# Hybrid attention and recurrence block on one core: token sums of the Strassen-Winograd up product formed after the turning instead of before it, with three small moves

## The reference

```
u = rmsnorm(h) * attn_norm_w
proj = u @ w_in                 # q,k,v of 8 attention heads; q, two gates, v, g of 4 recurrent heads
mix = concat(neighbourhood_attention(...), hgrn2_bidirectional(...))
h = h + mix @ w_out
u = rmsnorm(h) * mlp_norm_w
a = square(relu(u @ w_up))      # 1024 -> 4096
h = h + a @ w_down              # 4096 -> 1024
```

## Time and profile before

| what | value |
|---|---|
| median of 3 runs | 1293.55 us (1292.2 to 1294.88) |
| profiled execution | 1293.81 us, span 1292.0 us |
| TensorE busy | 1274.4 us, 99% |
| VectorE busy | 845.6 us, 65% |
| ScalarE busy | 587.4 us, 45% |
| GpSimd busy | 473.9 us, 37% |
| granted TensorE clock | 1.000 |

### The profile page before, as it was taken

One profiled execution on the slowest core, in us unless ns is written; L12 is line 12 of the kernel. 1 busy time (PEld: TensorE's weight loads), 2 busy tenths in 40 slices (PEclk: granted clock), 3 DMA queues, 4 the chain that ended last, 5 costly groups with the idle time before them and its releaser, 6 DMA issues.

```text
span 1292.0 us, 17686 instructions
## 1 busy us (share of the span) xinstructions
PE 1274.4 (99%) x6432; PEld 1072.9 (83%) x6432; DVE 845.6 (65%) x1268; ACT 587.4 (45%) x1058; POOL 473.9 (37%) x259
## 2 busy tenths in 40 slices
PE   7999999999999999999999999999999999999998
PEld 6878888998888889878888788888888888888887
DVE  3537666641869686976486654554555888888885
ACT  6346766445536354350345554454453433433341
POOL 3241212115030503045135544444443544544452
PEclk9999999999999999999999999999999999999999
DMA  7341332222010202152311744544559463533423
GB/s 247 129 131 49 82 103 83 83 66 82 1 50 1 66 1 68 47 185 74 134 49 58 243 139 146 166 137 145 166 203 374 138 238 98 190 133 102 162 86 144
DMA packets 134469, 154.92 MB, mean 120 GB/s; under 512 B 11376, under 2 KB 89584, under 8 KB 134384
## 3 DMA queue, kind: packets, MB, share of 16 engines
q1 hardware_dynamic: 131216, 147.04, 35.7%
q10 hardware_dynamic: 3168, 6.75, 1.4%
HBM read 109.72 MB, written 44.04 MB: 119 GB/s over the span
## 4 chain that ended last, share of the span: by engine, by line
PE 92%; DVE 4%; ACT 1%; issue 1%; DMA 1%; POOL 0%; ACTq 0%; SPq 0%; DVEq 0%
PE bank L2359 8%; PE bank L2362 8%; PE bank L2363 8%; PE bank L2328 7%; PE bank L2331 7%; PE bank L2332 7%; PE bank L2070 6%; PE bank L2066 6%; PE bank L2069 6%; PE bank L2153 4%; PE bank L2289 2%; PE bank L2285 2%; PE bank L2288 2%; PE bank L1964 1%; PE bank L1966 1%
## 5 line engine op out<-in xcount | busy, mean ns | idle before, releaser
L885 POOL TENSOR_TENSOR w_hi<-stage,one_col 128x1024 fp32r<-128x1024 f32 x32 | 61.3, 1917 | 409.6 <-DVE scores L1615 176.4
L943 POOL TENSOR_TENSOR a_split<-a_raw,a_split 128x1024 fp32r<-128x1024 f32 x56 | 148.0, 2663 | 166.1 <-ACT a_split L1223 166.1
L2328 PE MATMUL bank<-set,w_hi 128*128 128x512 f32 x448 | 177.8, 397 | 0.7 <-DVE s L1860 0.6
L2331 PE MATMUL bank<-set,w_hi 128*128 128x512 f32 x448 | 176.1, 393 | 0.0
L2332 PE MATMUL bank<-set,w_lo 128*128 128x512 f32 x448 | 176.0, 393 | 0.0
L2359 PE MATMUL bank<-w_hi,a_split 128*128 128x512 f32 x448 | 174.6, 390 | 0.2
L2363 PE MATMUL bank<-w_hi,a_split 128*128 128x512 f32 x448 | 174.3, 389 | 0.0
L2362 PE MATMUL bank<-w_lo,a_split 128*128 128x512 f32 x448 | 174.3, 389 | 0.0
L2066 PE MATMUL bank<-uT_hi,w_hi 128*128 128x512 f32 x384 | 158.7, 413 | 0.0
L2070 PE MATMUL bank<-uT_hi,w_lo 128*128 128x512 f32 x384 | 150.5, 392 | 0.0
L2069 PE MATMUL bank<-uT_lo,w_hi 128*128 128x512 f32 x384 | 149.7, 390 | 0.0
(11 more groups left out here) (227 smaller groups left out, 2748.9 us busy)
## 6 DMA issues: line engine op xcount, KB each, us to landing
a_raw<-a_dram SPq DMA_DIRECT2D x56, 512.0 KB, 3.8
a_dram<-abuf SPq DMA_DIRECT2D x111, 256.0 KB, 2.1
stage<-in_w_in SPq DMA_DIRECT2D x29, 512.0 KB, 4.1
raw<-in_w_down SPq DMA_DIRECT2D x10, 1024.0 KB, 8.0
stage<-in_w_up SPq DMA_DIRECT2D x16, 512.0 KB, 5.1
raw_b<-in_w_up SPq DMA_DIRECT2D x16, 512.0 KB, 5.7
x_tok<-in_x SPq DMA_DIRECT2D x8, 512.0 KB, 8.5
v_dram<-vs ACTq DMA_DIRECT2D x16, 256.0 KB, 2.3
```

The lines of the kernel that those rows point to most:

```text
L943: pool.tensor_tensor(split_of(m, 1), a_raw[:, m % 4, :, :], split_of(m, 0).bitcast(F32), ALU.subtract).then_inc(b_lo, 1)
L2328: first = pe.matmul(dst, w[0], u[0], start=k == 0 and p in (1, 5, 6, 7), stop=False, skip_group_check=True)
L2331: pe.matmul(dst, w[0], u[1], start=False, stop=False, skip_group_check=True)
```

## The change

Four edits:

1. *First mean.* The first `qk_average` comes after four steps of the next projection instead of two.
2. *Late ring split.* GpSimd's split of tile 35 waits for `squares_lo` of the last head. All eight residual loads are issued ahead of tile 37's load, after both `o_done` and `o_mean`.
3. *Token sums in turned form.* Only the four raw quarters are turned, 16 groups: 8 in the output projection as before, 8 in the first two j = 0, 1 products of p = 2. ScalarE keeps a 32-bit copy of each group (`keep_turned`), and the sums are formed from copies and banks in turned form: sets 5 and 7 by VectorE from a bank and a copy (`t1_sums`, `t3_sums`), T2 by VectorE from two copies (`t2_sums`), set 4 by GpSimd from two copies (`t4_sums`). The hi and lo parts of sets 7, 5, 6, 3 and 4 are made from these SBUF tensors instead of a bank. A product of j = 0 waits for its set k step by k step. The order of p = 3 and 4 for j = 0 changes; GpSimd's token sums go.
4. *Up block's order.* At j = 2 VectorE does `up_results(2)` ahead of the weight sums of j = 3 for p = 7 and 5.

More of the change, by code:

```diff
@@ L1347, in _ @@
             for t in range(TT):
+                if t in (5, 6):
+                    for g in range(4 * t - 20, 4 * t - 16):
+                        keep_turned(g)
                 act.wait_ge(added, 32 + 2 * t + 2)
                 rms(1, t)
-                for g in {4: range(4), 5: range(4, 8)}.get(t, ()):
-                    take_set(g)
+                if t in (4, 5):
+                    for k in range(4):
+                        take_set(t - 3, k)
             keep_p1(0)
@@ L1825, in _ @@
-            for n in range(4, 8):
-                up_sum(n)
[L1827 to L1830, removed]
-            dve.tensor_tensor(low, high, low, ALU.subtract).then_inc(t13_sum, 1)
-            dve.wait_ge(t13_sum, 7)
-            dve.tensor_tensor(high, u_tok[:, TT - 1, HALF:D], high, ALU.subtract).then_inc(t13_sum, 1)
-            for t in range(3):
-                t2_sums(t)
@@ L1836, in _, with t1_sums @@
-            take_set(8)
-            t2_sums(3)
-            take_set(9)
-            for t in range(4):
-                take_set(10 + t)
-                t4_sums(t)
-            for g in range(14, 20):
-                take_set(g)
+                if 41 <= n < 45:
+                    for k in ((0, 1), (2, 3))[(n - 41) % 2]:
+                        take_set(1 if n < 43 else 2, k)
+            def t1_sums(k):
+                dve.wait_ge(y_raw, 9 + k)
+                dve.tensor_tensor(raw_part(5, k), bank[TURN_BANK[8 + k]][:, :], raw_part(1, k), ALU.subtract).then_inc(t1_sum, 1)
@@ new lines, in t3_sums, with t2_sums @@
+            def t3_sums(k):
+                dve.wait_ge(y_turned, 13 + k)
+                dve.tensor_tensor(raw_part(7, k), bank[TURN_BANK[12 + k]][:, :], raw_part(7, k), ALU.subtract).then_inc(t3_sum, 1)
+            def t2_sums(k):
+                dve.wait_ge(y_raw, 13 + k)
+                dve.wait_ge(y_lo, SET_AT[5] + k + 1)
+                dve.tensor_tensor(raw_part(6, k), raw_part(3, k), raw_part(5, k), ALU.subtract).then_inc(t2_sum, 1)
+            up_sum(4)
+            normalise_tokens(1, TT - 1)
@@ L1917, in _ @@
             up_results(0)
-            take_set(26)
-            take_set(27)
-            up_sum(13)
+            take_set(3, 2)
+            take_set(3, 3)
+            for k in range(4):
+                take_set(4, k)
             up_results(1)
@@ L2003, in turn_set @@
             def turn_set(g):
[L2005 to L2024 removed]
+                (t0, col), k = QUARTERS[g // 4], g % 4
[4 more added lines that the diff above has]
+                    pe.wait_ge(t1_sum, g - 11)
+                elif TURN_BANK[g] >= 4 and g >= 8:
+                    pe.wait_ge(y_raw, g - 3)
+                elif g >= 8:
                     pe.wait_ge(added, 48)
@@ L2334, in up_product @@
                         ins.then_inc(up_done, 1)
-                    if (j, p, k) in TURNED_AT:
-                        turn_set(TURNED_AT[(j, p, k)])
+                    for g in TURNED_AT.get((j, p, k), ()):
+                        turn_set(g)
             for n in range(7 * UPS):
```

102 lines of the change are left out of this document (18 added, 84 removed).

## The result

The changed kernel takes 1296.2 us (median of 12 executions, 1293.88 to 1297.14) against 1293.22 for the kernel before (12 executions of the same session, 1292.2 to 1296.54): ratio 1.0019, 95% interval 1.0010 to 1.0027, so 2.5 us slower by the ratio and 3.0 by the medians. The profiled execution took 1296.02 us, span 1294.2, against a span of 1292.0 before. The sign was right, and the time lies at the lower edge of the forecast's own range (1296.2 to 1300.2); the size was forecast at +5.1, about twice what came.

The account below looks back on a forecast made before the run. TensorE, busy 1274.4 of 1292.0 us, was taken as the bound. Transposes -5.3, first mean -1.0, late ring split +0.5 and port waits +10.9 gave +5.1: 1298.6 us, own range 1296.2 to 1300.2, wider range 1292.0 to 1302.5.

Parts of the forecast that it names:

- Transposes: On TensorE's path, twelve turned groups go at 0.44 us each: -5.3 us.
- First mean: Before the first head average, two more projection steps cover TensorE's wait: -1.0 us, bounds 0 and -1.1.
- Late ring split: At the last head's means, TensorE resumes earlier but late residual loads give it back: +0.5 us, between -0.5 and +1.5.
- The port: In the up block, VectorE's two-SBUF-input instructions and GpSimd's reads block each other, so TensorE waits: +10.9 us.
- Means near 1.9 us: Sign of being right: VectorE's remainders of sets 5, 6 and 4 average near 1.9 us where GpSimd works.
- Sum: Whole kernel: -5.3 - 1.0 + 0.5 + 10.9 = +5.1 us, 1298.6 us against the median.
- half of it: Rival: VectorE and GpSimd instructions meet less often, waits sum to 5 to 10 us, 1291 to 1296 us; chance 0.14.
- Without contention: Rival: set remainders from SBUF run beside GpSimd undisturbed, no waits arise, -7.3 in all, 1286.2 us; chance 0.14.
- the clock rival: Waits around 683 to 696 lower TensorE's clock for products (0,6) and (1,6): +2.5 us, 1301.1; chance 0.08.

Follow-up runs that it names:

- early weights: Changed kernel with set 4's sums on VectorE and weights of products number 5 to 10 prepared earlier; 1288.98 us, ratio 0.9964.
- the fills: Changed kernel with GpSimd's weight remainders of products number 6 to 13 and set 4 sums replaced by zero fills; 1286.1 us.
- all loads late: Kernel before with the late ring split and all eight residual loads behind the two means; ratio 1.0000, stretch 0.23 us longer.
- two means: Kernel before with the first and second mean products each after four projection steps instead of two; stretch 67.34 us, 0.2 us gained.
- turned form + order: Kernel before with the turned token sums and the up block's order only; up block 4.97 us longer, ratio 1.0040.
- old order: Changed kernel with j = 2's result adds back behind the two weight sums; block 1.33 us longer, 1.7 us slower by ratios to before.
- set 4 on VectorE: Changed kernel with the four sums for set 4 on VectorE, behind the T2 sums; block 1.93 us shorter, ratio 1.0004.
- filled wait: Changed kernel with ten more TensorE matmuls ahead of product (0,6), during its wait; ratio 1.0015 against 1.0019.

## Why the prediction was right or wrong

- **Transposes**, -5.3: the block less its waits is 86.53 us before and 81.57 with early weights, 0.41 us a group, **-5.0** (with the fills 81.15, so -5.4). Right.
- **First mean**, -1.0: measured **0.0**, my own lower bound. This is the smaller of the two steps that failed, the choice between the bounds: I named the chain behind the mean and then took the value that ignores it. The wait moved to the second mean.
- **Late ring split**, +0.5: measured **-2.7**. This is the main step that failed: "all residual loads now wait for the means". Three do not, and the first is still issued at 566.58. The sentence before it, that TensorE could resume near 570.3 instead of 572.92, was the right term. The run with all loads late, +0.2 against +0.5, shows that little else in it was off.
- **The port**, +10.9: waits went from 1.18 to 10.72, **+9.5**, at the products named. Drawn against measured: (0,5) 1.1 and 1.2 against 0.63 and 0.90; (0,6) 3.2 and 1.2 against 2.68 and 0.84; (0,3) 2.3 against 2.21 with the clock up, 0.82 and 1.37 of low clock with it down; (0,4) 0.3, 1.2 and 1.2 against 0, 0.83 and 0.89; (1,4) 0.5 against 0.52. A pair costs 1.70, not the 1.85 of the sum. Means near 1.9 us were named as the sign; the sixteen average 1.26, since only some of them meet an instruction of GpSimd. One is missed, (2,4): 0.2 drawn, 1.24 measured, since VectorE reaches the activation sums of j = 1 some 2 us later, measured by TensorE's pace, than before, and the result adds then stand right behind them. Taking rather than the earlier trace rows was the choice that decided the sign, and the fills show it.
- **Sum**: -5.0 + 9.5 + 0 - 2.7, unrounded +1.9, and 0.3 in gaps too small to count as waits; the span says +2.2, the ratio +2.5, the medians +3.0. Of the 2.9 us between forecast and span, the misread loads are 3.2, the mean -1.0, the block 0.7.
- **Rivals.** The time fell on the edge of *half of it* (1291 to 1296), but not by its mechanism: it wanted waits of 5 to 10 us, and 10.72 were there; the misread loads brought the time down. (The text there speaks of twelve waits; its list has ten, 12.4 us in sum.) Without contention the forecast was -1.5 - 5.3 in the block; with the fills it is 5.1 us shorter than before. The clock did fall where that rival put it, but for six matmuls and 1.37 us, not 24 and 4.8, and it cost nothing, not 2.5: the wait behind it, 2.21 us with the clock up, is longer and absorbs all of it.

## What to carry to other kernels

When an operand moves from a bank to SBUF, count the instructions of VectorE with two SBUF inputs that will meet a reading GpSimd, at 1.7 us a pair, and place GpSimd's work where VectorE reads banks: moving it (with set 4's sums on VectorE, 1.9 of it) was worth 7.7 us here, more than the 5.0 of the twelve groups. Read every wait in a diff against the instructions on both sides of it: two waits in a row in the text may have issues between them. A stall on the busiest engine, low clock included, costs only what the next wait behind it does not take back; giving one mean more time, when its successor's operands hang on it, wins nothing: the wait moves on.

## What had not been expected of the hardware

- After one and the same wait of 1.98 us ahead of the last head's means, the kernel before and the one with the first mean alone kept their pitch (95.76 us in the second column), while the profiles of two others with that code unchanged (two means; turned form + order) took 97.20 and 97.30: matmuls at 0.43 us for a while, 1.5 us lost. My argument against the clock rival, that this wait had left the pitch at 0.23, rested on one execution. In the up block the clock fell behind the wait of 2.68 us (also in the turned form with the order and in the changed kernel with the old order) and behind one of 2.03 (set 4 on VectorE), but not behind 1.81 (the same kernel), 2.21 (filled wait) or 2.59 (old order, ahead of (2,4)). So the length of a wait alone does not tell. The late ring split takes away the wait of 1.98, and with it this occasional 1.5 us: the stretch is 93.10 in all nine profiles that have it.
- The 100th matmul starts between 28.3 and 31.4 us in the fourteen profiles, though no code ahead of it differs. That is as much as most effects here, so a difference of two spans of less than these 3 us says little until it is split into stretches. Whether the spread of one kernel's times lies there too is not shown, since each kernel has one profile, and why it moves was not looked into.
